# Twenty of 22 feature blocks of each up projection by Strassen's scheme in a hybrid decoder layer

## The reference

```
x = x + 1/2 * SwiGLU(RMSNorm(x))        # first FFN, D_FF = 2816
x = x + concat(A, B) @ W_out            # token mixer: 4 heads of mLSTM and 4 pooling groups
x = x + 1/2 * SwiGLU(RMSNorm(x))        # second FFN
return RMSNorm(x)
def swiglu(h, w_gate, w_up, w_down):
    return (silu(h @ w_gate) * (h @ w_up)) @ w_down
```

## Time and profile before

| | |
|---|---|
| median of 3 runs | 952.6 us (951.3 to 952.77) |
| span of the profiled execution, first to last instruction | 949.3 us |
| TensorE matmuls | 928.4 us busy, x4232 |
| VectorE | 488.3 us busy |
| ScalarE | 295.1 us busy |
| GpSimd | 58.3 us busy |
| DMA | 91.62 MB, mean 97 GB/s |

### The profile page before, as it was taken

The page is one execution under the profiler, slowest core; times in us unless marked ns, Lnnn a source line. Parts: engine busy times, 40 slices in busy tenths (PEclk is TensorE's granted clock), DMA queues, the critical chain, the costliest instruction groups (busy, mean ns, idle before and its releaser), DMA issues.

```text
span 949.3 us, 11415 instructions
## 1 busy us (share of the span) xinstructions
PE 928.4 (98%) x4232; PEld 770.5 (81%) x4232; DVE 488.3 (51%) x716; ACT 295.1 (31%) x374; POOL 58.3 (6%) x75
## 2 busy tenths in 40 slices
PE   8999999999999999999989999999999999999995
PEld 5888888888888888888877888888888888888884
DVE  6655444555433434677887665445544455433324
ACT  5222222222222323545762443222222222223220
POOL 5000000000000000001345100000000000000002
PEclk9999999999999999999999999999999999999997
DMA  6423332223333233122212132322333223333312
GB/s 199 134 88 98 110 101 88 88 88 110 111 112 103 99 108 110 67 90 82 65 53 68 67 110 72 107 88 88 106 104 99 88 88 91 130 109 100 102 45 89
DMA packets 28475, 91.62 MB, mean 97 GB/s; under 512 B 3120, under 2 KB 6448, under 8 KB 28448
## 3 DMA queue, kind: packets, MB, share of 16 engines
q1 hardware_dynamic: 28272, 90.79, 29.2%
q0 software_dynamic: 176, 0.46, 0.2%
HBM read 89.14 MB, written 2.10 MB: 96 GB/s over the span
## 4 chain that ended last, share of the span: by engine, by line
PE 92%; DVE 3%; ACT 3%; DMA 1%; issue 1%; SPq 1%; DVEq 0%; ACTq 0%
PE ps L253 30%; PE ps L254 30%; PE ps L255 30%; PE ps L286 1%; DMA x<-x_t 1%; ACT w_hi L602 1%; ACT arena L733 0%; ACT arena L728 0%; DVE act_lo L1106 0%; SPq L221 0%; DVE act_lo L1150 0%; ACT L717 0%; ACT L728 0%; DVE x L1267 0%; DVE tcol L933 0%
## 5 line engine op out<-in xcount | busy, mean ns | idle before, releaser
L253 PE MATMUL ps<-xg_hi,w_hi 128*128 128x512 f32 x840 | 329.9, 393 | 3.0 <-DVE xg_lo L906 2.2
L254 PE MATMUL ps<-xg_lo,w_hi 128*128 128x512 f32 x840 | 327.6, 390 | 0.0
L255 PE MATMUL ps<-xg_hi,w_lo 128*128 128x512 f32 x840 | 327.6, 390 | 0.0
L602 ACT ACTIVATE w_hi<-raw 128x1024 fp32r<-128x1024 f32 x163 | 171.8, 1055 | 342.4 <-PE ps L255 182.4
L901 DVE TENSOR_TENSOR w_lo<-raw,w_hi 128x1024 fp32r<-128x1024 f32 x163 | 200.8, 1232 | 133.4 <-ACT w_hi L602 133.3
L253 PEld LDWEIGHTS ps<-xg_hi,w_hi 128*128 128x128 f32 x840 | 158.2, 188 | 38.8 <-issue 3.1
L255 PEld LDWEIGHTS ps<-xg_hi,w_lo 128*128 128x128 f32 x840 | 158.1, 188 | 33.3
L254 PEld LDWEIGHTS ps<-xg_lo,w_hi 128*128 128x128 f32 x840 | 158.2, 188 | 32.1
L253 PE MATMUL ps<-act_hi,w_hi 128*128 128x512 f32 (+1 forms) x438 | 166.0, 379 | 0.2 <-DVE act_lo L1180 0.2
L254 PE MATMUL ps<-act_lo,w_hi 128*128 128x512 f32 (+1 forms) x438 | 165.7, 378 | 0.0
L255 PE MATMUL ps<-act_hi,w_lo 128*128 128x512 f32 (+1 forms) x438 | 165.7, 378 | 0.0
(11 more groups left out here) (140 smaller groups left out, 503.5 us busy)
## 6 DMA issues: line engine op xcount, KB each, us to landing
raw<-weights SPq DMA_DIRECT2D x162, 512.0 KB, 3.3
x<-x_t SPq DMA_DIRECT2D x8, 256.0 KB, 5.9
out<-x SPq DMA_DIRECT2D x6, 256.0 KB, 2.2
raw<-weights SPq DMA_DIRECT2D x9, 128.0 KB, 5.7
out<-x SPq DMA_DIRECT2D x4, 128.0 KB, 2.0
raw<-weights SPq DMA_DIRECT2D x1, 384.0 KB, 2.8
arena<-pool_w POOLq DMA_DIRECT2D x1, 256.0 KB, 6.2
vec<-vecs SPq DMA_DIRECT2D x1, 73.5 KB, 2.0
```

What stands on the lines that cost most here:

```text
L253: pe.matmul(acc, hi, m_hi, start=first, stop=False)
L254: pe.matmul(acc, hi, m_lo, start=False, stop=False)
L255: return pe.matmul(acc, lo, m_hi, start=False, stop=last)
L602: act.activation(w_hi[:, k % SLOTS], raw[:, k % RAWS], ACT.Copy).then_inc(hi_made, 1)
```

## The change

Blocks 0 and 1 of each up stage stay as they were (PLAIN = 2). For the other 20 (NS), gate and up block, the two halves of the 1024 inputs and the two halves of the 512 tokens make a 2 x 2 by 2 x 2 product of blocks: weights A (two feature blocks by two input halves, quarters of 128 x 512), operand B (input half by token half). It is done in Winograd's form of Strassen's scheme, in seven products of 12 matmuls with 256 columns instead of eight. Factors of the weights are A11, A12, A22 themselves (products 1, 2, 4) and four sums S1 to S4 (products 5, 6, 7, 3); factors of the operand are B11, B21 and B22 (products 1, 2, 3) and the sums T1 to T4 (products 5, 6, 7, 4), made once for each stage by `x_terms`, one round for each of the KH = 4 tiles of an input half.

What moves with it. The weights of Strassen blocks are loaded in quarters of 256 KB, with one raw buffer for each of the four. Weight factors live in half slots of w_hi and w_lo; only that of product 4 has two places. The operand of the plain blocks goes to spare room in act_hi and act_lo. Copies of partial results (p1, p5, u2) from PSUM are ScalarE's, and so is the rounding of the activations, before DVE's. Up is no longer multiplied by rinv: DVE multiplies the output of the down stage by it instead. Loads of pool_w wait until the first down unit has been used. `last_block`'s reciprocal root works on the two columns of its half.

The core of the diff: TensorE's products, x_terms on ScalarE, x_terms on DVE, the down stage's update of x, and SP's loop. In it p is the FFN (0 or 1), s the Strassen block, par its parity.

```diff
+            def product(i, s, par, acc, first=False):
+                pe.wait_ge(f_lo[i], s + (p * NS + 1))
+                hi, lo = factor(i, par, p)
+                for k in range(KH):
+                    at = slice(k * P, (k + 1) * P)
+                    m_hi, m_lo = moving(i, k)
+                    pe.matmul(acc, hi[:, at], m_hi, start=first and k == 0, stop=False, skip_group_check=True)
+                    pe.matmul(acc, hi[:, at], m_lo, start=False, stop=False, skip_group_check=True)
+                    mm = pe.matmul(acc, lo[:, at], m_hi, start=False, stop=k == KH - 1, skip_group_check=True)
+                mm.then_inc(p_done[i], 1)
+            def last_two(s, par, steps):
+                if 3 in steps:
+                    pe.wait_ge(p5_copied, s + (p * NS + 1))
+                    product(3, s, par, ps_c[par])
+                if 4 in steps:
+                    pe.wait_ge(c22_made, s + (p * NS + 1))
+                    product(4, s, par, ps_b[par])
+            def period(s, par, early=False, head=False):
+                if head:
+                    pe.wait_ge(b11_made, 2 * (p + 1))
+                    pe.wait_ge(te_made, 2 * KH * (p + 1))
+                if not early:
+                    pe.wait_ge(prod_made, s + (p * FB + PLAIN - 1))
+                product(1, s, par, ps_b[par], True)
+                if not early:
+                    pe.wait_ge(c12_made, s + (p * NS - 1))
+                product(5, s, par, ps_c[par], True)
+                if not head:
+                    last_two(s - 1, 1 - par, (3,))
+                pe.wait_ge(p1_copied, s + (p * NS + 1))
+                product(6, s, par, ps_b[par])
+                if not head:
+                    last_two(s - 1, 1 - par, (4,))
+                if head:
+                    pe.wait_ge(rinv_made, stage + 1)
+                else:
+                    pe.wait_ge(c11_made, s + p * NS)
+                product(2, s, par, ps_a, True)
+                pe.wait_ge(u2_copied, s + (p * NS + 1))
+                product(7, s, par, ps_b[par])
+            for f in range(PLAIN):
+                plain(f)
+            period(0, 0, early=True, head=True)
+            period(1, 1, early=True)
+            with pe.Fori(1, NS // 2) as it:
+                period(it * 2, 0)
+                period(it * 2 + 1, 1)
+            last_two(NS - 1, 1, (3, 4))
...
+            def x_terms(k):
+                if k > 0:
+                    act.wait_ge(t_step, 4 * (p * KH + k))
+                act.activation(rinv[:], x[:, k], ACT.Copy, scale=scalar_of(V_GAIN + stage * KD + k)).then_inc(b1_made, 1)
+                act.wait_ge(t_step, 4 * (p * KH + k) + 1)
+                act.activation(xg_hi[:, k, HALF:T], tt[:, 0:HALF], ACT.Copy).then_inc(t_hi_made, 1)
+                act.wait_ge(t_step, 4 * (p * KH + k) + 4)
+                act.activation(xe_hi[:, :, k], tt[:, HALF:].rearrange("p (a n) -> p a n", n=HALF), ACT.Copy).then_inc(t_hi_made, 1)
...
+            def x_terms(k):
+                dve.wait_ge(b1_made, p * KH + k + 1)
+                if k > 0:
+                    dve.wait_ge(te_made, 2 * (p * KH + k))
+                dve.tensor_tensor(t1, b12, b11, ALU.subtract).then_inc(t_step, 1)
+                dve.scalar_tensor_tensor(t3, x22, far, b12, ALU.mult, ALU.subtract).then_inc(t_step, 1)
+                dve.wait_ge(t_step, at + 2)
+                dve.tensor_tensor(t2, t3, b11, ALU.add).then_inc(t_step, 1)
+                dve.wait_ge(t_step, at + 3)
+                dve.scalar_tensor_tensor(t4, x21, far, t2, ALU.mult, ALU.subtract).then_inc(t_step, 1)
+                dve.wait_ge(t_hi_made, 2 * (p * KH + k) + 1)
+                dve.tensor_tensor(xg_lo[:, k, HALF:T], t1, f32(xg_hi[:, k, HALF:T]), ALU.subtract).then_inc(te_made, 1)
+                dve.wait_ge(t_hi_made, 2 * (p * KH + k) + 2)
+                dve.tensor_tensor(xe_lo[:, :, k], tt[:, HALF:].rearrange("p (a n) -> p a n", n=HALF),
+                                  f32(xe_hi[:, :, k]), ALU.subtract).then_inc(te_made, 1)
...
-                    dve.scalar_tensor_tensor(x[:, d], ps[:, 4 + d % banks], factor, x[:, d], ALU.mult, ALU.add).then_inc(x_new, 1)
+                    dve.tensor_tensor(work[:, d % 2], acc_of(d), rinv[:], ALU.mult).then_inc(y_scaled, 1)
+                    dve.wait_ge(y_scaled, KD * (stage == 3) + d + 1)
+                    dve.scalar_tensor_tensor(x[:, d], work[:, d % 2], 0.5, x[:, d], ALU.mult, ALU.add).then_inc(x_new, 1)
...
+                with sp.Fori(1, NS) as s:
+                    sp.wait_ge(s_made[3], s + p * NS)
+                    load_block(p, s, 2)
+                    sp.wait_ge(f_lo[1], s + p * NS)
+                    load_block(p, s, 0)
+                    sp.wait_ge(f_lo[4], s + p * NS)
+                    load_block(p, s, 3)
+                    sp.wait_ge(f_lo[2], s + p * NS)
+                    load_block(p, s, 1)
```

More of the change, by code:

```diff
@@ L201, in f32, with plain_x, factor, block_of @@
             return ap.bitcast(F32)
+        def plain_x(k, part):
+            spare, own = (act_hi, xg_hi) if part == 0 else (act_lo, xg_lo)
+            return spare[:, XP + k] if k < KH else own[:, k]
+        def factor(i, par, p):
+            h = PLACE[i] + (par if i == 4 else 0)
+            s = (AFTER[p] + h // 2) % SLOTS
+            at = slice((h % 2) * T, (h % 2 + 1) * T)
+            return w_hi[:, s, at], w_lo[:, s, at]
+        def block_of(p, j):
+            return raw[:, (AFTER[p] + j // 2) % RAWS, (j % 2) * T:(j % 2 + 1) * T]
         def first_part(i):
@@ L324, in step, with moving @@
                     for i in range(2):
[L325 to L331, removed]
+                        n = base + 2 * f + i
+                        column_block(n, n, ps[:, 2 * f + i], before(2 * f + i), plain=True)
+                def moving(i, k):
+                    if i in T_OF:
+                        return xe_hi[:, T_OF[i], k], xe_lo[:, T_OF[i], k]
+                    k = k + KH if i in (2, 3) else k
+                    at = slice(HALF, T) if i in (3, 5) else slice(0, HALF)
+                    return xg_hi[:, k, at], xg_lo[:, k, at]
@@ new lines, in ffn_up @@
+                x_terms(0)
+                x_terms(1)
+                inverse_rms(stage)
+                x_terms(2)
+                x_terms(3)
+                dve.wait_ge(unit_used, base + 1)
+                sum_1(0)
+                sum_3(0, True)
+                sum_2(0)
+                lo_of(1, 0, 0)
+                lo_of(5, 0, 0)
+                take_rinv(stage)
+                plain_gate(0)
+                lo_of(6, 0, 0)
+                sum_4(0, True)
+                plain_product(0)
@@ new lines, in ffn_up @@
+                lo_of(2, 0, 0)
+                act_low(0)
+                lo_of(7, 0, 0)
+                plain_gate(1)
+                plain_product(1)
+                lo_of(4, 0, 0)
+                act_low(1)
+                iteration(0, 0, head=True)
+                iteration(1, 1)
+                with dve.Fori(1, NS // 2 - 1) as it:
+                    iteration(it * 2, 0)
+                    iteration(it * 2 + 1, 1)
+                iteration(NS - 2, 0)
+                iteration(NS - 1, 1, tail=True)
@@ L986, in out_blocks @@
+                gate(NS - 1, 1)
+                split_lo(q + 2, q + 2)
+                product(NS - 1, 1)
+                act_low(FB - 1)
+                split_lo(q + 3, q + 3)
+                clear_squares(stage + 1)
+            def out_blocks(base, per, stage, acc_of, scaled):
                 for d in range(KD if stage < 3 else KD - 1):
```

405 lines of the change are left out of this document (313 added, 92 removed).

## The result

The changed kernel takes 960.14 us (median of 4 runs, 959.29 to 960.42) against 952.68 us for the kernel before on the same chip (4 runs, 951.3 to 952.77): ratio 1.0081, 95% interval 1.0067 to 1.0095, slower by 7.5 us. Forecast were 956.7 us and slower at 0.57. The profiled span grew from 949.3 to 958.6 us, by 9.3 where 4.1 were forecast.

A forecast was written before the change was run, and what follows sets the result against it. TensorE, busy 98% of the span, was taken to bound the kernel. First up stage +6.3, second -2.6 and the end +0.4 sum to +4.1 us, giving 956.7 against the median 952.6; range 946 to 974.

The forecast's parts named there:

- Steady period: Strassen loop of the up stages: 10.12 us per block, bounds 10.08 and 10.83.
- rival 2: Strassen loop: DMA load of a quarter in control, period 10.33 to 10.83, total 965 to 984 us; chance 0.14.
- +6.3: First up stage: ends 6.3 us later than before, at 259.7 instead of 253.4.
- -2.6: Second up stage: ends 2.6 us earlier than before, at 811.1 instead of 813.7.
- (a): Head of each up stage: four x_terms rounds on ScalarE and DVE, 3.7 us a round.
- (b): Head of each up stage: chain from sum_1 of block 0 to ScalarE's copy of its p1, 13.5 us.
- Rival 1: Head: shorter than walked, x_terms rounds 2.7 us instead of 3.7, total 948.7 us; chance 0.22.
- rival 4: Head: waits (b) fall short, (a) stays and the clock holds, about 952 us, no change; chance 0.10.
- The clock: Head of each up stage: TensorE's clock falls to 1.2 GHz behind the long waits, 2.5 us lost per head.
- Rival 3: Strassen loop: TensorE pays 0.09 us at seven product waits a period, +24 us, total 981; chance 0.06.
- The tail's +0.4: End of the kernel: DVE's scaling behind the last down half, 256 columns with a wait, adds 0.4 us.
- The mixer's zero: Into the mixer: an extra 0.7 us of scaling on block 7's chain is covered and costs nothing.

The follow-up runs named there:

- without quarter 3's wait: Against the changed kernel, sum_1 adds quarter 2 to itself, so no sum waits for quarter 3 (result partly altered): 948.41 us.
- lengthened: Against the changed kernel, SP issues quarter 3's load after lo 2 instead of after lo 4: 1018.07 us.
- the early copies: Against the changed kernel, ScalarE's copies of p1 and u2 of block 0 moved ahead of act_high(0) and silu(1): 959.04 us.
- with the clock held up: Against the changed kernel, sixty unused 256-column matmuls ahead of product 6 of block 0 in each stage: 957.83 us.
- one exchange: Against the changed kernel, sum_3 put before sum_1 in each iteration, SP's wait before quarter 2's load adjusted: 953.89 us.
- the tight version: Against the version with six plain blocks, head order tightened on ScalarE and DVE: 935.05 us; with sum_3 before sum_1 as well, 931.32 us.
- the other way to shorten the same loop: Against the tight version, DVE makes lo 4 before the product of the block before, instead of behind it: 943.24 us.

## Why the prediction was right, and where it was off

Direction and mechanism held: the head gives back what TensorE saves. The other signs came as well: VectorE busy 95 to 97% in the loop, a wait of 5.25 us at the replicate for about 6, two of 7.87 and 7.88 at product 6, and the clock of 0.50 behind them. That the total came within 3.5 us of the forecast is in part luck. In the period, TensorE's own 10.00 for 10.08 made up for more than half of a loop that costs 0.14 to 0.17 and not 0.04; at the head, 5 us booked for the clock stood where a wait for VectorE stands that the sum did not follow.

- **TensorE's saving.** 0.80 us a block was forecast; its own period of 10.00 makes it 0.88, 35 us in all. The 0.1200 of the earlier trace rows was read in a down stage; in the up stage without waits it is 0.119.
- **Steady period.** Forecast 10.12, measured 10.17 and 10.14. The mechanism is rival 2's, which I held at 0.14 as deciding only from 10.33: the loop does have control (without quarter 3's wait 10.00, lengthened 11.80), but at a size near the lower bound. The term mis-sized is landing, 2.7 for 2.3 from the slope of 512 and 384 KB. In the period from 139.37 the loop is 7.30 from sum_1's start to lo 4's end at 146.67 (forecast 7.29), 0.17 to SP's issue at 146.84, 2.66 to the landing at 149.50 and 0.09 to the next sum_1: 10.22. The walk through the period also left out the one place where TensorE pays for it, product 1's wait for VectorE's product; "TensorE waits for none" held only without the loop.
- **The page's price.** The Trainium skill's fit in "DMA: Bandwidth & Descriptors", section "Anatomy of one DMA", which the page gives for transfers issued by GpSimd, had given 2.6 and a loop of 10.13. The row of the kernel after, 2.7 for SyncE's transfers, and the page agree, and my slope through two points did not.
- **The first period.** I priced all 19 alike. Measured 10.93 and 11.50, since lo 4 of block 0 comes late in the head and sum_1(1) waits 2.13 us behind it: the loop's delay in full where no earlier period has filled it. The 18 intervals from 65.65 and from 626.11 take 183.75 and 183.85 us where 10.12 each makes 182.2; of the 1.6 and 1.7 us more, 0.8 and 1.4 are this first one. They are nearly all of +8.2 against +6.3 and of -1.0 against -2.6.
- **The head.** (a) 3.85 us a round for 3.7, (b) 13.56 for 13.5, from sum_1's start at 43.57 to the end of the copy at 57.13; product 6 at 57.18 for 57.3. In the second stage it is 618.2 at the shifted forecast of 618.4 (608.7 + 9.75, by which the stage began later). Rival 1 (a round under 2.95) and rival 4 are out. Two sums of the walk are off: the parts listed for a round make 3.43, not 3.7, and VectorE's own make 2.9, not 2.7. Of the measured 3.85 VectorE stands 0.65 for ScalarE, so 3.2 are its own, above rival 1's limit even if ScalarE's part had hidden. That the wait at product 6 was the cost was too narrow, though: with it removed the time stayed (the early copies).
- **The clock.** 2.5 us were lost in the records as forecast, but the sum booked them on the path; with the clock held up the heads gave 0.8 us, not 5. VectorE's chain to block 1's low parts, which the sum did not follow, holds TensorE at the same place without the clock's fall: the copy of p1 of block 2 is at 76.58, and with the clock held up at 76.67. These two errors cancelled.
- **Rival 3** is out: without the loop TensorE takes 84 x 0.119 to 0.01 us, through twelve waits a period.
- **The rest.** The tail's +0.4 came to 0.6. The mixer's zero came to +1.6 by a fall of the clock (below); the scaling that moved into that chain added nothing, since in the kernels without that fall the same stretch takes 304.03 to 304.08, and 304.07 before.

## What to carry to other kernels

A scheme that trades matmuls for vector work is paid for at its head, where no earlier block covers the vector work: run the old form until the new form's inputs are ready, which here, together with the earlier inverse_rms, turned +0.8% into -1.2%. Then look for the loop through a single-buffered load and put every instruction that does not need that load ahead of the one that waits for it; one exchange gave 0.6% (0.4% in the tight version), while the other way to shorten the same loop crossed a bank's deadline and lost 0.9%. A long wait in the profile says where a chain ends, not which part of it to shorten.

## What the runs showed of the hardware that was not expected

TensorE's granted clock fell inside the mixer, in code that is the same in all these kernels: 0.81 and 0.85 over 500 to 510 us in the kernel after, 0.66 over 500 to 505 with sum_3 first, and 0.69 over 495 to 500.5 with four plain blocks. In the timeline of PE of the kernel after:
```profile
503.06 0.59 PE L341 MATMUL ps<-xg_hi,w_hi 128*128 128x512 f32 x1
...
506.00 0.63 PE L342 MATMUL ps<-xg_lo,w_hi 128*128 128x512 f32 x1
```
From 503.06 to 506.71 nine matmuls start, most 0.43 apart instead of 0.23, which costs about 1.6 us; the stretch from the first x row to W_out's end is 305.63, 305.66 and 305.94 in the three kernels with a fall and 304.03 to 304.08 in the nine others. TensorE had stood 1.04 us just before, up to 500.70, and then run eight matmuls of one column and six of 512 at the full pace. The kernel before and the eight other variants, with the same instructions there, keep 1.00 throughout the mixer. Each kernel was profiled in one execution, so whether the fall belongs to the kernel or to the execution is not shown. What decides it stays open; no run was made for it.
